# Constant products on TensorE at the head of each attention unit

## The chip, the cores and the metric

The kernel runs on one core of one Trainium2 chip. The metric is the time of one launch in microseconds of device time; lower is better. PE is TensorE, DVE is VectorE, ACT is ScalarE, POOL is GpSimd, SP is SyncE.

## What is computed

Three model blocks are applied one after the other to an activation of 1024 tokens by 1024 channels, in float32: an attention over chunks with a spatial gating unit, gates and a feed-forward; an mLSTM beside a windowed attention with a feed-forward; and a convolution beside a neighbourhood attention. The change touches the first and the third attention.

```python
# first block: 8 heads of 64, each chunk of 64 sees its own and 8 previous chunks
scores = jnp.einsum('bcqhd,bckhd->bhcqk', qc, kb).astype(jnp.float32) * (Dh ** -0.5)
scores = scores + bias[None, :, None, :, :]
scores = jnp.where(valid[None, None, :, None, :], scores, jnp.float32(-1e30))
probs = jax.nn.softmax(scores, axis=-1).astype(v.dtype)
out = jnp.einsum('bhcqk,bckhd->bcqhd', probs, vb)
...
# third block: 8 heads of 64, a grid of 16 rows by 64 columns, a window of 8 rows by 16 columns
s = jnp.einsum("bhwd,bhiwjd->bhwij", q_row, k_win).astype(jnp.float32) * scale
s = s + bias.transpose(0, 2, 1, 3).astype(jnp.float32)[None]
p = jax.nn.softmax(s.reshape(B, N_HEADS, GRID_W, kh * KW), axis=-1)
...
return jnp.einsum("bhwij,bhiwjd->bhwd", p, v_win)
```

## The kernel before

Activations are kept transposed, channels on partitions, as 8 tiles of 128 by 1024. A weight product is made of three products of rounded parts (w_hi with x_hi, w_hi with x_lo, w_lo with x_hi), so a *block* of 128 output features is 8 tiles by 3 parts by 2 halves of 512 tokens, 48 matmuls at line 389 (`feature_block`, `row_block`) or line 407 (`block_part`, a block cut in three). SP loads the weight blocks, POOL splits them into w_hi and w_lo, PE takes them in order.

PE writes into two accumulators, `acc[0]` and `acc[1]`, of 1024 columns each, in turn. `claim` waits until the accumulator of this turn has been taken, and `await_all_taken` until both have. The other half of PSUM holds `turned` (three banks for turned probabilities) and `att_out`.

Both attentions run over four *units* of two heads (a head pair). The names from here on:

- The **projections** of a unit are its weight blocks for v, q and k (and a gate in the third). ACT copies each from PSUM. In the third attention the units after the first also add eight row products of the unit before to `h` (`near_rows`, `add_rows`, line 897 on DVE).
- Then PE waits in `await_all_taken` until both accumulators are free: this is the **head pause**.
- `att_tensor` then runs over eight query tiles p = 0 to 7 of 128 queries. **S(p)** (line 709, `score`) is the scores of tile p for the two heads of the unit, one head per accumulator, on 64 rows of the array each. The number of keys is 128, 256, 384, 512 and then 640 in the first attention, and 512, 512, four times 576, and twice 512 in the third. **T(p)** (line 720, `turn_probs`) turns the probabilities, and **V(p)** (line 744, `weigh_values`) weighs the values with them. PE's order is S(0), S(1), T(0), S(2), T(1), V(0), S(3), T(2), V(1), and so on. At S(p+1) PE claims both accumulators, so it waits until DVE has taken both heads of S(p).
- DVE (`att_vector`) adds the bias and takes the row minimum (line 813, two of them per tile), ACT takes the exponential (line 854), DVE divides by the sum (lines 823 and 826), PE turns, ACT copies (line 864). DVE's own order is: scores of p, division of p, scores of p+1.
- After the last tiles a block of projections is cut into the pipeline to fill it (line 407).

DVE also works on the taps of the third block's convolution (line 1733), a fixed number of them between two units of the third attention.

TensorE's clock falls to half in stretches, which the profile lists. The kernel already has a function against that, `keep_clock`, that makes products of constants whose result nobody reads:

```python
def keep_clock(pe, n):
    for _ in range(n):
        pe.matmul(acc_all[:, 2 * TOK:2 * TOK + P], mean_w[:, :], ident[:, :], start=True, stop=True)
```

Both operands are 128 by 128 in float32, and the output is the first bank of `turned`. It is called at the norms, and at four other places between stages, and nowhere in the first or the third attention.

Of the kernel before, what the change touches and what calls it, by code (L numbers as in the profile page):

```python
# [155 lines left out]
def mixer_program(nc, x_t, blocks, n_blocks, params, consts, bias_1, bias_2, bias_3, sgu_rows, sgu_w, p_t,  # L156
                  out_t):

    with ExitStack() as ctx:
        def at(name, kib, shape, dtype=F32):  # L160
            return nc.alloc_sbuf_tensor_at(name, shape, dtype, offset=RESERVED + int(kib * 1024))
# [21 lines left out]
        def attention_buffers(base, kib, probs_kib, bias_kib, bias_width):  # L183
            return Buffers(
                q_t=at(base + "q_t", kib, [P, TOK]), k_t=at(base + "k_t", kib + 4, [P, TOK]),
                v_tok=at(base + "v_tok", kib + 8, [P, TT, P]), v_t=at(base + "v_t", kib + 12, [P, TOK]),
                scores=at(base + "scores", kib + 12, [P, 2, 640]),
                probs_t=at(base + "probs_t", kib + 17, [P, 2, 2, 5, P]),
                total=at(base + "att_sum", kib + 27, [P, TOK]), probs=at(base + "probs", probs_kib, [P, 2, 2, 640]),
                bias=at(base + "bias", bias_kib, [P, 2, bias_width]))  # L190

        band = attention_buffers("band_", 88, 152, 190, ATT_BIAS_1)
# [68 lines left out]
        near = Buffers(  # L261
            q_t=at("near_q_t", 140.625, [P, TOK]), k_t=at("near_k_t", 144.625, [P, TOK]),
            v_tok=at("near_v_tok", 148.625, [P, TT, P]), v_t=at("near_v_t", 156.625, [P, TOK]), scores=None,
            probs=at("near_probs", 152.625, [P, 2, 2, 640]), probs_t=at("near_probs_t", 162.625, [P, 2, 2, 5, P]),
            total=at("near_att_sum", 172.625, [P, TOK]), bias=None)
# [95 lines left out]
        def await_all_taken(e, t):  # L361

            for s in range(2):
                e.wait_ge(acc_free[s], t.count(f"acc{s}"))


        def take_block(pe, t):

            pe.wait_ge(w_split, t.next("block"))
            t.block += 1  # L370
            return (t.block - 1) % 2
# [25 lines left out]
        def feature_block(pe, t, parts_from=None):  # L397

            slot = take_block(pe, t)
            product(pe, t, [(slot, k, x_hi[:, k, :], x_lo[:, k, :]) for k in range(KT)], True, parts_from)  # L400
# [101 lines left out]
# [3 lines that stand above are left out]
# [175 lines left out]

        def att_tensor(pe, t, a, keys, next_block=True, joint=False):

            ahead = 1 if joint else 0

            def rows_of(side):
                return slice(64 * side, 64 * side + 64)

            def score(p):  # L690

                first, count, _ = keys(p)
                if joint:
                    s = claim(pe, t)
                    take_turn(pe, t)
                    for side in range(2):
                        ins = pe.matmul(acc[s][:, side * HALF:side * HALF + count],
                                        a.q_t[rows_of(side), p * P:(p + 1) * P],
                                        a.k_t[rows_of(side), first:first + count], start=True, stop=True)
                    ins.then_inc(acc_full[s], 1)  # L700
                    return
                slots = []
                for _ in range(2):
                    slots.append(claim(pe, t))
                    take_turn(pe, t)
                for c0 in range(0, count, 512):
                    c1 = min(count, c0 + 512)
                    for side in range(2):
                        ins = pe.matmul(acc[slots[side]][:, c0:c1], a.q_t[rows_of(side), p * P:(p + 1) * P],  # L709
                                        a.k_t[rows_of(side), first + c0:first + c1], start=True, stop=True)  # L710
                        if c1 == count:
                            ins.then_inc(acc_full[slots[side]], 1)

            def turn_probs(p):

                count = keys(p)[1]

                def turn(bank, side, c, at):
                    w = min(P, count - c * P)
                    return pe.transpose(turned[bank][0:w, at * P:(at + 1) * P],  # L720
                                        a.probs[:, p % 2, side, ahead + c * P:ahead + c * P + w], ident[:, :])

                for side in range(2):
                    pe.wait_ge(p_ready, t.next("p_ready"))
                    for _ in range(0 if p == 0 else 2 if side and keys(p - 1)[1] > HALF else 1):
                        pe.wait_ge(turned_copied, t.next("turned_copied"))
                    for c in range(min(4, -(-count // P))):
                        ins = turn(side, side, c, c)
                    ins.then_inc(turned_full, 1)
                if count > HALF:  # L730
                    for side in range(2):
                        ins = turn(2, side, 4, side)
                    ins.then_inc(turned_full, 1)

            def weigh_values(p):
                first, count, _ = keys(p)
                tiles = -(-count // P)
                if p == TT - 1:
                    for _ in range(3 if count > HALF else 2):
                        pe.wait_ge(turned_copied, t.next("turned_copied"))  # L740
                for c in range(tiles):
                    w = min(P, count - c * P)
                    for side in range(2):
                        ins = pe.matmul(att_out[rows_of(side), p % 4 * P:(p % 4 + 1) * P],  # L744
                                        a.v_tok[0:w, first // P + c, rows_of(side)],
                                        a.probs_t[0:w, p % 2, side, c, :], start=(c == 0), stop=(c == tiles - 1))
                if p % 4 == 3:
                    ins.then_inc(pv_done, 1)

            for n in range(ahead):  # L750
                score(n)
            for n in range(TT + 2):
                if n + ahead < TT:
                    score(n + ahead)
                if n == TT and next_block:
                    slot, s = take_block(pe, t), claim(pe, t)
                    take_turn(pe, t)
                    block_part(pe, t, slot, s, 0, 3)
                if 1 <= n <= TT:
                    turn_probs(n - 1)  # L760
                if n >= 2:
                    if n == TT + 1 and next_block:
                        block_part(pe, t, slot, s, 3, 4)
                    weigh_values(n - 2)
            if next_block:
                block_part(pe, t, slot, s, 4, KT)
# [137 lines left out]
        def projections_tensor(pe, t):  # L904

            turn_tiles(pe, t, band.v_t)
            feature_block(pe, t)
            await_all_taken(pe, t)

        def qkv_scalar(act, t, a):  # L910
# [6 lines left out]
        def att1_tensor(pe, t):  # L917
            feature_pair(pe, t, expect_parts(t, KT))
            with t.loop(2, acc0=20, acc1=20, block=6, p_ready=32, turned_copied=40, hi_ready=2, lo_ready=2):
                for _ in range(2):  # L920
                    projections_tensor(pe, t)
                    att_tensor(pe, t, band, keys_1)
                    feature_block(pe, t)
                    t.next("hi_ready")
                    t.next("lo_ready")
# [845 lines left out]
        def near_rows(pe, t):  # L1771
            await_parts(pe, t, 1)
            row_block(pe, t, [(near_hi[:, :], near_lo[:, :])])

        def near_tensor(pe, t):
            feature_block(pe, t)
            for n in range(HEAD_PAIRS):
                if n:
                    group_sums(pe, t, (n - 1, 0), n - 2 if n > 1 else None, near_square[:, :], t.next("squared"))
                feature_block(pe, t)  # L1780
                turn_tiles(pe, t, near.v_t)
                feature_block(pe, t)
                feature_block(pe, t)
                if n:
                    near_rows(pe, t)
                await_all_taken(pe, t)
                att_tensor(pe, t, near, keys_3)

        def conv_tensor(pe, t):
            last_near = t.next("squared")  # L1790
# [559 lines left out]
```

## Time and profile before

| | |
|---|---|
| median of 3 runs | 3624.6 us (3622.15 to 3625.77) |
| the profiled execution, its own time | 3623.64 us |
| its span | 3621.9 us |
| mean granted TensorE clock | 0.985 of full speed |
| PE busy | 3478.8 us (96%) |
| DVE busy | 1728.9 us (48%) |
| ACT busy | 797.4 us (22%) |
| POOL busy | 1201.0 us (33%) |

The span is the time from the first to the last instruction of one execution; the run's own time has 1.7 us more around it. Times in rows are us from the start of the span. The granted clock is 1.00 at 2.4 GHz and 0.50 at 1.2 GHz; there are no other levels in this trace. A row of the timeline merges instructions that follow each other, and its duration goes from the first one's start to the last one's modelled end.

### The profile page before, as it was taken

The numbers are of one execution on the slowest core, as the hardware profiler recorded it, in microseconds if no ns is written. First come the engines' busy times: TensorE is split into PE (matmuls) and PEld (weight loads), VectorE is DVE, ScalarE is ACT, GpSimd is POOL, SyncE is SP. The second block draws the span as 40 slices with busy tenths as digits, with TensorE's granted clock in tenths as the row PEclk, the third lists the DMA queues.
The fourth block names the chain that finished last, engine by engine and source line by source line (L and its number), as shares of the span: only waits on it lengthen the run. The fifth ranks groups of instructions, "written<-read, shape, count | busy, mean of one in ns | idle before, by whom it ended". The sixth has DMA issues, their size and how long they took to land.

```text
span 3621.9 us, 41941 instructions
## 1 busy us (share of the span) xinstructions
PE 3478.8 (96%) x16940; PEld 2772.5 (77%) x16940; DVE 1728.9 (48%) x2073; ACT 797.4 (22%) x1170; POOL 1201.0 (33%) x534
## 2 busy tenths in 40 slices
PE   7999999989999999989999999999999999999997
PEld 5767877778888888777876678888888868767675
DVE  4323433352323223588866642322322368888835
ACT  4433100020000000332234430000000141333452
POOL 2222344323433433333321134334333424222222
PEclk9999999999999999999999999999999999999998
DMA  2111211111111111122111011111111101111111
GB/s 95 39 36 38 93 47 46 47 35 47 46 52 46 46 52 46 35 66 81 59 34 33 23 41 47 52 46 46 52 46 58 47 18 60 59 60 58 44 35 64
DMA packets 52163, 178.96 MB, mean 49 GB/s; under 512 B 5728, under 2 KB 6368, under 8 KB 52064
## 3 DMA queue, kind: packets, MB, share of 16 engines
q1 hardware_dynamic: 38016, 138.43, 11.7%
q10 hardware_dynamic: 14048, 39.10, 3.2%
q8 instruction: 75, 1.23, 0.1%
q14 instruction: 24, 0.20, 0.0%
HBM read 172.79 MB, written 4.72 MB: 49 GB/s over the span
## 4 chain that ended last, share of the span: by engine, by line
PE 85%; DVE 8%; ACT 3%; issue 3%; POOL 1%; DMA 0%; ACTq 0%; DVEq 0%; POOLq 0%
PE acc L389 69%; PE acc L407 4%; PE acc L744 2%; PE acc L720 2%; PE acc L709 2%; PE acc L426 2%; DVE conv_slots L1733 1%; PE acc L473 1%; DVE rstd L618 1%; DVE normed L650 1%; DVE x_lo L488 0%; DVE h L897 0%; POOL w_lo L2060 0%; DVE window_scores L777 0%; PE acc L1355 0%
## 5 line engine op out<-in xcount | busy, mean ns | idle before, releaser
L2046 POOL TENSOR_TENSOR w_hi<-raw,zero 128x1024 fp32r<-128x1024 f32 x264 | 515.6, 1953 | 2365.2 <-PE acc L389 1663.1
L389 PE MATMUL acc<-x_hi,w_hi 128*128 128x512 f32 x2512 | 778.4, 391 | 5.7 <-POOL w_lo L2060 3.0
L389 PE MATMUL acc<-x_lo,w_hi 128*128 128x512 f32 x2512 | 774.2, 389 | 0.0
L389 PE MATMUL acc<-x_hi,w_lo 128*128 128x512 f32 x2512 | 774.0, 389 | 0.0
L2060 POOL TENSOR_TENSOR w_lo<-raw,w_hi 128x1024 fp32r<-128x1024 f32 x262 | 678.9, 2591 | 20.5
L897 DVE TENSOR_TENSOR h<-h,acc 128x1024 f32<-128x1024 f32 x312 | 380.7, 1221 | 554.9 <-PE acc L389 554.9
L389 PEld LDWEIGHTS acc<-x_hi,w_hi 128*128 128x128 f32 x2512 | 470.0, 188 | 106.7 <-POOL w_lo L2060 4.7
L389 PEld LDWEIGHTS acc<-x_lo,w_hi 128*128 128x128 f32 x2512 | 471.9, 188 | 98.7
L389 PEld LDWEIGHTS acc<-x_hi,w_lo 128*128 128x128 f32 x2512 | 471.8, 188 | 98.5
L1164 DVE TENSOR_TENSOR hid<-act_g,acc 128x1024 f32<-128x1024 f32 x44 | 53.7, 1221 | 570.7 <-PE acc L389 554.7
L483 ACT ACTIVATE hid_hi<-hid 128x1024 fp32r<-128x1024 f32 x44 | 46.7, 1061 | 909.2 <-DVE hid L1164 909.2
L1733 DVE SCALAR_TENSOR_TENSOR conv_slots<-conv_slots,par 128x1024 f32<-128x1024 f32 x120 | 227.8, 1898 | 4.1
L389 PE MATMUL acc<-hid_hi,w_hi 128*128 128x512 f32 x704 | 217.0, 389 | 0.7 <-DVE hid_lo L488 0.7
L389 PE MATMUL acc<-hid_lo,w_hi 128*128 128x512 f32 x704 | 216.7, 389 | 0.0
L389 PE MATMUL acc<-hid_hi,w_lo 128*128 128x512 f32 x704 | 216.7, 389 | 0.0
L488 DVE TENSOR_TENSOR hid_lo<-hid,hid_hi 128x1024 fp32r<-128x1024 f32 x44 | 138.2, 3140 | 49.9 <-ACT hid_hi L483 49.9
L389 PEld LDWEIGHTS acc<-hid_hi,w_hi 128*128 128x128 f32 x704 | 131.9, 188 | 28.5 <-DVE hid_lo L488 1.1
L389 PEld LDWEIGHTS acc<-hid_lo,w_hi 128*128 128x128 f32 x704 | 132.1, 188 | 27.5
L389 PEld LDWEIGHTS acc<-hid_hi,w_lo 128*128 128x128 f32 x704 | 132.1, 188 | 27.4
L1140 ACT ACTIVATE act_g<-acc 128x1024 f32<-128x1024 f32 x44 | 45.3, 1029 | 360.2 <-PE acc L389 360.1
L504 PEld LDWEIGHTS acc<-ident,mean_w 128*128 128x128 f32 x812 | 95.0, 194 | 21.0 <-issue 20.2
L504 PE MATMUL acc<-ident,mean_w 128*128 128x128 f32 x812 | 95.5, 278 | 16.2 <-DMA h<-x_t 16.2
(332 smaller groups left out, 4068.9 us busy)
## 6 DMA issues: line engine op xcount, KB each, us to landing
raw<-blocks SPq DMA_DIRECT2D x264, 512.0 KB, 3.4
near_bias<-bias ACTq DMA_DIRECT2D x16, 512.0 KB, 4.0
h<-x_t ACTq DMA_DIRECT2D x8, 512.0 KB, 8.2
h<-x_t ACTq DMA_DIRECT2D x1, 4096.0 KB, 15.5
q_past<-q_dram ACTq DMA_DIRECT2D x8, 512.0 KB, 5.6
w_own<-r_dram ACTq DMA_DIRECT2D x8, 512.0 KB, 6.5
out_t<-out_rows ACTq DMA_DIRECT2D x8, 512.0 KB, 3.0
band_bias<-bias ACTq DMA_DIRECT2D x4, 640.0 KB, 4.1
```

The costliest lines, as they stand in the source:

```text
L389: ins = pe.matmul(acc[s][:, c], w[:, slot, tile, :], part[:, c], start=(n == 0 and m == 0), stop=(n == last and m == 2))
L407: ins = pe.matmul(acc[s][:, c], w[:, slot, k, :], part[:, k, c], start=(k == 0 and m == 0), stop=(k == KT - 1 and m == 2))
L426: ins = pe.matmul(acc[accs[b]][:, c], w[:, slots[b], k, :], part[:, k, c], start=(k == 0 and m == 0), stop=(k == KT - 1 and m == 2))
L488: dve.tensor_tensor(lo, source, hi.bitcast(F32), ALU.subtract).then_inc(lo_ready, 1)
L504: pe.matmul(acc_all[:, 2 * TOK:2 * TOK + P], mean_w[:, :], ident[:, :], start=True, stop=True)
L709: ins = pe.matmul(acc[slots[side]][:, c0:c1], a.q_t[rows_of(side), p * P:(p + 1) * P], a.k_t[rows_of(side), first + c0:first + c1], start= ...
L720: return pe.transpose(turned[bank][0:w, at * P:(at + 1) * P], a.probs[:, p % 2, side, ahead + c * P:ahead + c * P + w], ident[:, :])
L744: ins = pe.matmul(att_out[rows_of(side), p % 4 * P:(p % 4 + 1) * P], a.v_tok[0:w, first // P + c, rows_of(side)], a.probs_t[0:w, p % 2, si ...
L897: dve.tensor_tensor(h[:, j, :], h[:, j, :], acc[s], ALU.add).then_inc(acc_free[s], 1)
L1733: ins = dve.scalar_tensor_tensor(out=out, in0=shifted, scalar=weight, in1=out, op0=ALU.mult, op1=ALU.add)
L2046: pool.tensor_tensor(hi, whole, nothing, ALU.add).then_inc(hi_split, 1)
L2060: pool.tensor_tensor(lo, whole, hi.bitcast(F32), ALU.subtract).then_inc(w_split, 1)
```

## The change

`att_tensor` takes a pair `idle`. After S(0) it makes `idle[0]` constant products and after S(1) `idle[1]`. Ahead of `await_all_taken`, in the head pause, come 12 products in the first attention and 10 in the third. The pairs are (9, 3) in the first and (18, 8) in the third. The second attention calls `att_tensor` with the pair (0, 0). No wait, semaphore, transfer or buffer changes. With four units in each attention this is 4 x (12 + 9 + 3) + 4 x (10 + 18 + 8) = 240 products more.

```diff
-        def att_tensor(pe, t, a, keys, next_block=True, joint=False):
+        def att_tensor(pe, t, a, keys, next_block=True, joint=False, idle=(0, 0)):
...
             for n in range(TT + 2):
                 if n + ahead < TT:
                     score(n + ahead)
+                if n < 2:
+                    keep_clock(pe, idle[n])
...
             turn_tiles(pe, t, band.v_t)
             feature_block(pe, t)
+            keep_clock(pe, 12)
             await_all_taken(pe, t)
...
                     projections_tensor(pe, t)
-                    att_tensor(pe, t, band, keys_1)
+                    att_tensor(pe, t, band, keys_1, idle=(9, 3))
...
                 if n:
                     near_rows(pe, t)
+                keep_clock(pe, 10)
                 await_all_taken(pe, t)
-                att_tensor(pe, t, near, keys_3)
+                att_tensor(pe, t, near, keys_3, idle=(18, 8))
```

## Rows read from the trace of the kernel before

**Rows 1.** The page: its first line, and the shares by engine of the chain that ended last.

```profile
span 3621.9 us, 41941 instructions
...
PE 85%; DVE 8%; ACT 3%; issue 3%; POOL 1%; DMA 0%; ACTq 0%; DVEq 0%; POOLq 0%
```

**Rows 2.** Windows: stretches of lowered clock in both attentions; stretch, busy us, granted clock.

```profile
74.09:80.92 6.83, 6.28 (x22) 2.41 (x20) 5.07 (x22) 3.58 (x14) 0.00 (x0) 0.50 0.01 2
...
207.21:210.62 3.41, 3.41 (x16) 1.51 (x12) 2.90 (x12) 2.27 (x10) 0.00 (x0) 0.50 0.00 0
...
3313.34:3320.17 6.83, 5.81 (x18) 3.00 (x20) 4.96 (x17) 4.00 (x10) 0.00 (x0) 0.50 0.39 99
...
sum 40.97, PE 36.73 PEld 17.75 DVE 31.17 ACT 21.73 POOL 0.00; mean PE 4.59 PEld 2.22 DVE 3.90 ACT 2.72 POOL 0.00
```

**Rows 3.** Groups by line, 740.7 to 745.5 us, where the kernel calls `keep_clock(pe, 20)`.

```profile
L504 PE MATMUL acc<-ident,mean_w 128*128 128x128 f32 x40 | 4.6, 275 | 0.0
```

**Rows 4.** Timeline of PE, third unit of the first attention: start, duration, [idle before].

```profile
200.95 0.61 PE L389 MATMUL acc<-x_lo,w_hi 128*128 128x512 f32 x2
201.40 0.61 PE L389 MATMUL acc<-x_hi,w_lo 128*128 128x512 f32 x2
203.22 0.49 PE L709 MATMUL acc<-band_k_t,band_q_t 64*128 64x128 f32 x4 [1.21 <-ACT band_k_t L914]
204.62 0.70 PE L709 MATMUL acc<-band_k_t,band_q_t 64*128 64x256 f32 x4 [0.91 <-DVE small L813]
...
206.75 1.24 PE L709 MATMUL acc<-band_k_t,band_q_t 64*128 64x384 f32 x4 [0.63 <-DVE small L813]
...
212.95 1.35 PE L709 MATMUL acc<-band_k_t,band_q_t 64*128 64x512 f32 x8 [0.34 <-DVE small L813]
...
216.30 1.35 PE L709 MATMUL acc<-band_k_t,band_q_t 64*128 64x512 f32 x8 [0.17 <-DVE small L813]
```

**Rows 5.** Timeline of DVE in the same unit.

```profile
203.94 0.35 DVE L813 CUSTOM_DVE_ANT_0 band_scores<-acc,band_bias,small 128x128 f32<-128x128 f32 x1
...
205.80 0.48 DVE L813 CUSTOM_DVE_ANT_0 band_scores<-acc,band_bias,small 128x256 f32<-128x256 f32 x1
```

**Rows 6.** Timeline of PE, first unit of the first attention: S(0) and S(4).

```profile
72.41 0.49 PE L709 MATMUL acc<-band_k_t,band_q_t 64*128 64x128 f32 x4 [1.21 <-ACT band_k_t L914]
...
82.93 1.35 PE L709 MATMUL acc<-band_k_t,band_q_t 64*128 64x512 f32 x8 [0.34 <-DVE small L813]
```

**Rows 7.** Timeline of PE, first unit of the third attention.

```profile
3120.97 0.61 PE L389 MATMUL acc<-x_hi,w_lo 128*128 128x512 f32 x2
3122.88 1.13 PE L709 MATMUL acc<-near_k_t,near_q_t 64*128 64x512 f32 x4 [1.30 <-ACT z_att L1831]
3125.85 2.08 PE L709 MATMUL acc<-near_k_t,near_q_t 64*128 64x512 f32 x4 [1.84 <-DVE small L813]
...
3129.78 1.30 PE L709 MATMUL acc<-near_k_t,near_q_t 64*128 64x512 f32 x8 [0.28 <-DVE small L813]
3131.14 1.11 PE L720 MATMUL acc<-ident,near_probs 128*128 128x128 f32 x8
...
3133.20 1.30 PE L709 MATMUL acc<-near_k_t,near_q_t 64*128 64x512 f32 x8
```

**Rows 8.** Timeline of DVE in the same unit: last division of tile 0, first scores of tile 1.

```profile
3126.82 0.49 DVE L826 TENSOR_SCALAR near_probs<-near_probs,small 128x512 f32<-128x512 f32 x1
...
3128.20 0.75 DVE L813 CUSTOM_DVE_ANT_0 near_probs<-acc,near_bias,small 128x512 f32<-128x512 f32 x1
```

**Rows 9.** Timeline of PE, third unit of the third attention: last row products, S(0) and S(3).

```profile
3309.35 0.63 PE L389 MATMUL acc<-near_hi,w_lo 128*128 128x512 f32 x2
3311.39 1.13 PE L709 MATMUL acc<-near_k_t,near_q_t 64*128 64x512 f32 x4 [1.40 <-DVE h L897]
...
3322.50 1.30 PE L709 MATMUL acc<-near_k_t,near_q_t 64*128 64x512 f32 x8
```

**Rows 10.** The chain that ended last, between two units of the third attention: start, us, what.

```profile
3182.77 1.87 DVE near_lo L488
3184.64 3.35 DVE conv_slots L1733
```

## The prediction, made before the change was run

> **What bounds the kernel now.** I read the page first. The chain that ended last is PE for 85% [rows 1], so PE time that is removed or added at a place where PE or its answer is waited for is removed from or added to the end. A change that adds work to PE alone and gives no shorter path of its own can only gain through the clock. So the second view is the granted clock. I cut the trace into its stretches of lowered clock: eight of them, one in each unit, lie in the two attentions, and together they last 40.97 us [rows 2]. In each unit the clock falls shortly after the head pause: PE has just waited for ACT or DVE, made the small S(0), and waited again for DVE, and then the clock is at 1.2 GHz for 3.41 or 6.83 us. The first attention has 6.83 twice and then 3.41 twice, the third 3.41 twice and then 6.83 twice. PE's work takes twice as long there, so no more than half of 40.97 us, 20.5 us, is to be had.
>
> The third view is the timeline of single heads, where one sees how long each pause is and who ends it. In the third unit PE's 512-column products come in pairs 0.45 us apart, so after the pair at 201.40 PE is free at 201.85, and S(0) starts at 203.22: a head pause of 1.37 us. S(0) holds PE for about 0.33 us (its four instructions last 0.49 to the modelled end), and S(1) starts 1.40 after S(0): a second pause of 1.07 us [rows 4]. The first unit of the third attention is free at 3121.42 and starts S(0) at 3122.88, a pause of 1.46 us. Its S(0) of 512 keys holds PE for about 0.97 us (1.13 to the end), and S(1) is 2.97 later: a second pause of 2.00 us [rows 7]. In the units after it PE is free at 3309.81 and starts at 3311.39, 1.58 us [rows 9].
>
> **What the change adds.** It removes and moves nothing. What counts is how long one constant product is. The kernel has the same call elsewhere: twenty products are 40 matmul instructions, since one float32 product of 128 columns is issued as two, and the 40 keep PE busy for 4.6 us with 0.275 for one [rows 3]. So they start (4.6 - 0.275) / 39 = 0.111 us apart, which with the rounding I take as 0.112, and one product is 0.224 us at full clock. At half clock it would be up to 0.448, but the clock is 1.00 when each head begins.
>
> The Trainium skill bears on this price. Its page TensorE: Matmul & The Clock Gate, section Back-to-back issue gap, gives 128 / 2.4 + 2.5 = 56 ns from one 128-column matmul to the next at 2.4 GHz, and by that all of these products would fit into their pauses. The row of this kernel has two instructions of 112 ns for each product, four times as much, and I go by the row.
>
> *Head pause.* 12 products are 2.69 us in a pause of 1.37: S(0) starts 1.32 us later. In the third attention 10 products are 2.24 us: 0.78 later in its first unit, 0.66 in each of the other three. ACT and DVE have long finished and wait, so nothing hides this. Sum: 4 x 1.32 + 0.78 + 3 x 0.66 = 8.0 us.
>
> *First attention from S(0) to S(4), at full clock throughout.* After S(0) come 9 products, 2.02 us, so S(1) starts at 0.33 + 2.02 = 2.35 instead of 1.40. S(1) lasts 0.70, and DVE starts on a result 0.23 us after it is there (203.94 against 203.71). So DVE takes the scores of tile 1 at 3.28, before at 2.58 [rows 4, 5], and S(2), which waits for both takings, moves by the same 0.70 from 3.53 to 4.23. The 3 products behind S(1) end at 2.35 + 0.53 + 0.67 = 3.55; T(0) fits in before S(2), so they are hidden. If DVE were faster they would cost up to 0.67. From S(2) on the pace is DVE's: S(1) to S(2) takes 2.13 for 128 columns divided and 256 scored, S(4) to S(5) takes 3.35 for 512 and 640. In between, by columns, S(2) to S(3) takes 2.54 and S(3) to S(4) 2.94 at full clock, an estimate from these two rows; with 3.41 us of half clock the two took 6.20 together. So S(4) is at 4.23 + 5.48 = 9.71. Before it was at 9.73 in the third unit [rows 4] and at 10.52 in the first [rows 6]; the second and the fourth are as their neighbours. Gain 0.8 twice and nothing twice: 1.6 us.
>
> *Third attention from S(0) to S(3).* 18 products are 4.03 us behind 0.97: S(1) at 5.00 instead of 2.97. S(1) holds PE until 5.97. 8 products, 1.79, end at 7.76, and T(0), eight turns at the 0.11 of [rows 7], at 8.64. Only then can S(2) start, before at 6.90. DVE is not the later one here: S(1) is there at 6.13, DVE starts at 6.36, and its two scorings with what lies around them took 1.58 (3128.20 to 3129.78), so the accumulators are free at 7.94 [rows 7, 8]. From S(2) PE makes S(2), T(1) and V(0) in a row, 3.42 us [rows 7], so S(3) is at 12.06. Before it was at 10.32 in the first two units and 11.11 in the third and fourth [rows 7, 9]. Loss 2 x 1.74 + 2 x 0.95 = 5.4 us.
>
> *Where it goes from there.* The first attention ends in PE's own blocks. Between units of the third the chain runs from PE's projections over ACT to the division and split on DVE and then over convolution taps [rows 10]; their number is fixed and they start when the attention has ended, so a late unit is late in full. Weights are no cover either: POOL and SP follow PE's use.
>
> **Sum.** 8.0 - 1.6 + 5.4 = 11.8 us. Against the profiled execution's own 3623.64 that is 3635.4; that execution lies 1.0 below the median of the runs, so by the median it is 3636.4. I predict 3636.4 us. "Same" means within 0.2%, 7.2 us, here and below, about what a measurement of this kernel can tell from no change.
>
> **Bounds of what the trace doesn't show.** How S(0) and the products follow each other (64 rows, then 128) is in no row; at each of the 16 places it can cost nothing or, an estimate, one more start of an instruction, 0.11 us: 0 to 1.8 us. I take nothing. The clock's return is worth between nothing (the DVE pace of 6.20 stays: 3 us more in the first attention) and what DVE's pace allows. Where the lowered stretches fall differs by execution; each unit has 3.41 or 6.83. If all eight had 6.83, before would be about 3 us longer and so the loss smaller. My own range for the forecast is 3631 to 3641.
>
> **Rivals.**
>
> *The products fit, and the clock's gain is what remains (faster).* For this a product must cost what one instruction does, 0.112 us: 12 of them are 1.34 in 1.37, 9 are 1.01 in 1.07, 10 are 1.12 in 1.46, and 18 are 2.02 in 2.00. Then S(4) in the first attention is at 3.53 + 5.48 = 9.01, a gain of 1.5 twice and 0.7 twice, 4.4 us. In the third DVE is free at 3126.82 + 0.49, 4.43 after S(0) [rows 8], takes tile 1 about then, S(2) follows 1.58 later at 6.05 and S(3) at 9.47: a gain of 0.85 twice and 1.64 twice, 5.0. Together 9.4 us: 3615.2. It turns at about 0.17 us for a product. For it speaks that 12, 9 and 18 at 0.112 fill the pauses to within 0.07 us; against it [rows 3]. By the 56 ns of the Trainium skill's page TensorE: Matmul & The Clock Gate the time would be this one too. Chance 0.10.
>
> *The loss is partly absorbed (same).* The clock falls less elsewhere, or DVE catches up in the 576-key tiles of the third attention, where PE and DVE end almost together. If half of the 5.4 us there and 3 of the first attention come back, 3630. Chance 0.17.
>
> *The clock falls all the same, only later in the unit (slower still).* PE still has pauses around S(2) and S(3) of the first attention, of 0.63 before S(2) [rows 4]. Then the change pays for the products and gives back none of the 9.4 us: about 3645. Against it: in all eight units the fall comes right behind the pauses that are now filled. Chance 0.10.
>
> That leaves 0.63 for the forecast. Faster by over 0.2% is the first rival, 0.10. Same gets the second rival and a little of the low end of the forecast, 0.19; slower the rest, 0.71. The range reaches down to the absorbed loss and up towards the third rival: 3626 to 3643.
>
> **What the profile after would show.** Groups of line 504 with 24, 18 and 6 instructions in the first attention and 20, 36 and 16 in the third, 480 more in all, 0.112 apart. S(0) directly behind them, without idle time. S(1) 2.35 after S(0) in the first attention and 5.0 in the third. No stretch of lowered clock between S(0) and S(4). S(4) at 9.7 and S(3) at 12.1. A T(0) in the third attention that starts at 7.8 and an S(2) that waits for nothing. The prediction is wrong if a product takes one instruction, if the clock still falls, or if S(3) of the third attention isn't later than 11.

## The result, and the profile after

| | median | range | ratio to the kernel before, 95% interval |
|---|---|---|---|
| before | 3622.73 us | 3619.8 to 3625.77, 6 runs | |
| changed | 3636.23 us | 3634.75 to 3637.99, 6 runs | 1.0037 (1.0024 to 1.005) |

The change makes the kernel slower by 13.5 us, 0.37%, clear of 0.2%; the prediction was 3636.4 us. The profiled execution took 3634.75 us, 11.1 more than that of before. One execution of the kernel third_no_s1 below took 10783 us where the six others took 3631 to 3636; it is left out, and every other execution counts. The page after, its first lines and the chain that ended last [rows 1]:

```profile
span 3633.0 us, 42901 instructions
...
PE 3510.3 (97%) x17420; PEld 2815.3 (77%) x17420; DVE 1727.1 (48%) x2073; ACT 797.5 (22%) x1170; POOL 1201.4 (33%) x534
...
PE 86%; DVE 7%; issue 3%; ACT 3%; POOL 1%; DMA 0%; ACTq 0%; DVEq 0%; POOLq 0%
```

PE has 17420 matmul instructions, before 16940: the 240 products are 480 instructions, and as many weight loads. The chain is a little more PE.

The windows of the eight units from S(0) on (stretch, us, PE busy, granted clock), where there were eight lowered stretches [rows 2]:

```profile
74.00:84.50 10.50, 9.71 (x67) 1.00 0.01 3
140.40:150.90 10.50, 9.71 (x67) 1.00 0.00 0
206.90:217.40 10.50, 9.70 (x67) 1.00 0.01 2
273.30:283.80 10.50, 9.70 (x67) 1.00 0.00 0
3127.00:3140.00 13.00, 13.00 (x103) 1.00 0.31 87
3223.40:3236.40 13.00, 13.00 (x104) 1.00 0.29 86
3319.70:3332.70 13.00, 13.00 (x104) 1.00 0.30 87
3417.90:3430.90 13.00, 13.00 (x104) 1.00 0.29 88
```

The clock is at 2.4 GHz in all eight. The change does what it says, and in the windows of the third attention PE has no idle time left at all. What fills it is the products. The timeline of PE in the first unit of the first attention [rows 6]:

```profile
74.02 0.49 PE L709 MATMUL acc<-band_k_t,band_q_t 64*128 64x128 f32 x4
74.44 2.27 PE L504 MATMUL acc<-ident,mean_w 128*128 128x128 f32 x18
76.64 0.70 PE L709 MATMUL acc<-band_k_t,band_q_t 64*128 64x256 f32 x4
77.28 0.94 PE L504 MATMUL acc<-ident,mean_w 128*128 128x128 f32 x6
78.05 0.38 PE L720 MATMUL acc<-ident,band_probs 128*128 128x128 f32 x2
78.54 0.92 PE L709 MATMUL acc<-band_k_t,band_q_t 64*128 64x384 f32 x4
...
81.07 1.13 PE L709 MATMUL acc<-band_k_t,band_q_t 64*128 64x512 f32 x4 [0.34 <-DVE small L815]
```

S(1) now comes 2.62 us after S(0) and waits for nothing but the 18 instructions in front of it. And in the first unit of the third attention [rows 7]:

```profile
3127.03 1.13 PE L709 MATMUL acc<-near_k_t,near_q_t 64*128 64x512 f32 x4
3128.08 4.29 PE L504 MATMUL acc<-ident,mean_w 128*128 128x128 f32 x36
3132.30 1.13 PE L709 MATMUL acc<-near_k_t,near_q_t 64*128 64x512 f32 x4
3133.36 2.05 PE L504 MATMUL acc<-ident,mean_w 128*128 128x128 f32 x16
3135.25 1.04 PE L720 MATMUL acc<-ident,near_probs 128*128 128x128 f32 x8
3136.21 1.30 PE L709 MATMUL acc<-near_k_t,near_q_t 64*128 64x512 f32 x8
...
3139.52 1.30 PE L709 MATMUL acc<-near_k_t,near_q_t 64*128 64x512 f32 x8
```

S(1) is 5.27 after S(0), before 2.97. S(2) is at 9.18, before at 6.90, right behind T(0) and without any wait.

### The profile page after: what moved, and what is told of

Same layout as the page of the kernel before. It is cut to its first block, busy times and chain, and to the rows that moved or that the text cites. A ratio compares the mean times of both kernels' runs of the same rounds, so it can differ in the third digit from the quotient of the medians.

```text
span 3633.0 us, 42901 instructions
## 1 busy us (share of the span) xinstructions
PE 3510.3 (97%) x17420; PEld 2815.3 (77%) x17420; DVE 1727.1 (48%) x2073; ACT 797.5 (22%) x1170; POOL 1201.4 (33%) x534
## 4 chain that ended last, share of the span: by engine, by line
PE 86%; DVE 7%; issue 3%; ACT 3%; POOL 1%; DMA 0%; ACTq 0%; DVEq 0%; POOLq 0%
PE acc L389 70%; PE acc L407 4%; PE acc L744 2%; PE acc L720 2%; PE acc L504 2%; PE acc L426 1%; PE acc L473 1%; PE acc L709 1%; DVE rstd L618 1%; DVE normed L650 1%; DVE conv_slots L1736 1%; DVE x_lo L488 0%; POOL w_lo L2064 0%; DVE window_scores L779 0%; PE acc L1358 0%
## 5 line engine op out<-in xcount | busy, mean ns | idle before, releaser
L504 PEld LDWEIGHTS acc<-ident,mean_w 128*128 128x128 f32 x1292 | 150.9, 193 | 29.9 <-issue 27.9
L504 PE MATMUL acc<-ident,mean_w 128*128 128x128 f32 x1292 | 154.5, 278 | 16.6 <-DMA h<-x_t 16.6
```

## The experiments

Ten kernels. Each differs from the changed kernel only in the counts, or in what a product is, and each was run beside the kernel before on the same chip. The counts are written as head pause, (behind S(0), behind S(1)), for the first and for the third attention. In the changed kernel they are 12, (9, 3) and 10, (18, 8).

| kernel | first | third | median us | its kernel before | ratio, 95% interval |
|---|---|---|---|---|---|
| fit | 5, (3, 1) | 6, (8, 4) | 3612.4 | 3622.49 | 0.9971 (0.9962 to 0.9981) |
| turns | 12, (9, 3), half price | 10, (18, 8), half price | 3612.79 | 3622.49 | 0.9974 (0.9965 to 0.9984) |
| head_only | 12, (0, 0) | 10, (0, 0) | 3622.9 | 3622.49 | 1.0003 (0.9993 to 1.0012) |
| scores_only | 0, (9, 3) | 0, (18, 8) | 3627.04 | 3622.49 | 1.0013 (1.0003 to 1.0022) |
| third_no_s1 | 12, (9, 3) | 10, (18, 0) | 3632.51 | 3621.79 | 1.0031 (1.0019 to 1.0043) |
| first_only | 12, (9, 3) | none | 3626.47 | 3621.79 | 1.0011 (1.0002 to 1.002) |
| fit_no_s1 | 5, (3, 0) | 6, (8, 0) | 3610.95 | 3621.79 | 0.997 (0.9959 to 0.9981) |
| fit_first | 5, (3, 1) | none | 3617.04 | 3621.79 | 0.9985 (0.9976 to 0.9994) |
| fit_head | 5, (0, 0) | 6, (0, 0) | 3615.36 | 3622.44 | 0.9982 (0.9973 to 0.9991) |
| fit_s0 | 0, (3, 0) | 0, (8, 0) | 3609.08 | 3622.44 | 0.9964 (0.995 to 0.9977) |

**fit: as many products as the pauses hold.**

```diff
-            keep_clock(pe, 12)
+            keep_clock(pe, 5)
...
-                    att_tensor(pe, t, band, keys_1, idle=(9, 3))
+                    att_tensor(pe, t, band, keys_1, idle=(3, 1))
...
-                keep_clock(pe, 10)
+                keep_clock(pe, 6)
...
-                att_tensor(pe, t, near, keys_3, idle=(18, 8))
+                att_tensor(pe, t, near, keys_3, idle=(8, 4))
```

> The change with fewer products, so many as go into each pause at 0.224 us each and 0.1 us at each turn between 64 and 128 rows: 5, (3, 1) in the first attention and 6, (8, 4) in the third. My theory (the loss is the products' overrun, and the clock's return is worth 9.4 us): no stretch of lowered clock in the eight units, S(0) and S(1) where they were before (S(1) 1.40 and 2.97 after S(0)), S(4) of the first attention at 9.0 and S(3) of the third at 9.5, and 9.4 us less than the kernel before, about 3613. Rival (the clock's return is worth next to nothing, since DVE sets the pace): within 2 us of the kernel before. Rival (fewer products don't hold the clock): stretches of lowered clock stay, 3618 to 3623.

Measured 3612.4, 10.1 less than before. In the first unit of the third attention:

```profile
3119.21 1.13 PE L709 MATMUL acc<-near_k_t,near_q_t 64*128 64x512 f32 x4
3120.27 2.05 PE L504 MATMUL acc<-ident,mean_w 128*128 128x128 f32 x16
3122.25 1.13 PE L709 MATMUL acc<-near_k_t,near_q_t 64*128 64x512 f32 x4
...
3125.28 1.30 PE L709 MATMUL acc<-near_k_t,near_q_t 64*128 64x512 f32 x8
...
3128.70 1.30 PE L709 MATMUL acc<-near_k_t,near_q_t 64*128 64x512 f32 x8
```

S(1) is at 3.04 and S(3) at 9.49; in the first attention S(4) is at 9.0 in all four units. The granted clock is 1.00 from S(0) on in the windows of all units. By its trace S(4) and S(3) of the eight units are 8.8 us earlier together than before, 4.2 in the first attention and 4.6 in the third. So the clock's return is real and worth about what the estimate of 9.4 said, and the rival by which DVE's pace hides it falls.

**turns: the same counts at half the price.** The constant product becomes a transposition of the same constant, which is one instruction. `keep_clock` elsewhere stays as it is.

```diff
+        def turn_clock(pe, n):
+            for _ in range(n):
+                pe.transpose(acc_all[:, 2 * TOK:2 * TOK + P], mean_w[:, :], ident[:, :])
...
-                    keep_clock(pe, idle[n])
+                    turn_clock(pe, idle[n])
...
-            keep_clock(pe, 12)
+            turn_clock(pe, 12)
...
-                keep_clock(pe, 10)
+                turn_clock(pe, 10)
```

> The change with the same counts, but each product of the heads is a transposition of the same constant by the identity, one matmul instruction instead of two. So the price of a product is halved and nothing else. My theory: 0.11 us each, the pauses are filled but not overrun by more than 0.2 us, and if transpositions hold the clock the time is 9 us below the kernel before, about 3614. If they don't hold it, the clock falls as in the kernel before and the time is that of the kernel before, 3623. The Trainium skill, TensorE: Matmul & The Clock Gate, part 4, says that the clock doesn't rise for transpositions; by that the second. Rival (the loss isn't the products' length but the interruption of the scores by other weights): 3630 or more.

Measured 3612.79, 9.7 less than before. Same places, same counts and same order, and the loss is gone. PE in the first unit of the third attention, and the windows of that unit and of the first unit of the first attention:

```profile
3118.58 1.25 PE L508 MATMUL acc<-ident,mean_w 128*128 128x128 f32 x10
3120.04 1.13 PE L713 MATMUL acc<-near_k_t,near_q_t 64*128 64x512 f32 x4 [0.21 <-ACT z_att L1839]
3121.10 2.18 PE L508 MATMUL acc<-ident,mean_w 128*128 128x128 f32 x18
3123.21 1.13 PE L713 MATMUL acc<-near_k_t,near_q_t 64*128 64x512 f32 x4
```

```profile
73.00:83.00 10.00, 8.70 (x57) 1.00 0.01 2
...
3120.00:3130.00 10.00, 9.89 (x76) 1.00 0.40 113
```

Eighteen products are 2.18 us here and 4.29 in the changed kernel. This is the prediction's first rival made true: at one instruction each the counts fit, and the time is 9.7 us below its kernel before, where that rival had 9.4. The clock holds. This kernel changes the kind of instruction together with its price. That the kind isn't what matters is seen in fit, where the products are those of the changed kernel, only fewer, and the gain is about the same, 10.1.

**head_only and scores_only: the two parts of the change.** In the first the pairs are (0, 0), in the second the two calls in the head pause are left out.

> Only the products of the head pause (12 and 10), the pairs are (0, 0). My theory: S(0) is late by what it is late in the changed kernel, 1.42 us in the first attention and 0.88 and 0.76 in the third, 8.8 us together. If the clock then holds, its 9.4 us come back and the time is about that of the kernel before (3622). If the clock still falls behind S(0), 3631. Rival (the products behind S(0) and S(1) cost nothing since DVE is waited for there): the whole loss is here, about 3636.

> Only the products behind S(0) and S(1), (9, 3) and (18, 8), none in the head pause. My theory: S(0) not late; S(4) of the first attention at 10.0, S(3) of the third at 12.5, as in the changed kernel, if the clock holds: 7.2 us more than before, about 3630. If the clock still falls in some units, 2 us more for each pair of them. Rival (the loss is all in the head pause): at or below the kernel before.

head_only measured 3622.9: the overrun of the head pause and the clock's return cancel, as the theory says. In its trace the clock still fell in two of the eight units, for 3.4 us each:

```profile
209.80:213.20 3.40, 3.40 (x14) 1.51 (x12) 2.72 (x12) 2.08 (x9) 0.00 (x0) 0.50 0.00 0
3220.30:3223.70 3.40, 3.33 (x14) 2.45 (x14) 3.05 (x10) 2.17 (x6) 0.00 (x0) 0.50 0.63 178
```

scores_only measured 3627.04, 4.6 more than before (an interval of about 1 to 8 us) where 7.2 was expected. Its S(0) isn't late and S(4) and S(3) are at the 10.0 and 12.5 of the changed kernel, so the 7.2 are there in its heads, and they lie inside the interval. The two results, 0.4 and 4.6, don't add up to 13.5, because each part alone already brings the clock back and so has the gain of about 9.4 us in it; the whole change has it once. Their sum with 9.4 added is 14.4, near the 13.5. Both parts thus cost time. Neither rival, which put all of it into one of them, holds, but that of scores_only is excluded by the lower end of the interval alone, 1 us.

**first_only: the change in the first attention alone.**

```diff
-                keep_clock(pe, 10)
...
-                att_tensor(pe, t, near, keys_3, idle=(18, 8))
+                att_tensor(pe, t, near, keys_3)
```

> The change in the first attention alone: 12 and (9, 3). My theory: S(0) 1.42 late in each of four units, S(7) 0.26 us early in all of them together against the kernel before: 5.4 us more, about 3628. The rest of the change, 8 us, is the third attention's. Rival (most of the loss is in the first attention's head pause, the most overrun one): 3633 or more.

Measured 3626.47, 4.7 more than before (expected 5.4). By the medians the larger part of the loss, 8.8 us, is the third attention's.

**third_no_s1: without the 8 products behind S(1) of the third attention.**

```diff
-                att_tensor(pe, t, near, keys_3, idle=(18, 8))
+                att_tensor(pe, t, near, keys_3, idle=(18, 0))
```

> The changed kernel without the 8 products behind S(1) in the third attention: the pair (18, 0). My theory: those 8 products and T(0) stand in front of S(2) and set it at 9.19 after S(0). Without them DVE sets it: S(1) at 5.27 is there at 6.40, DVE starts at 6.69, S(2) at 8.27. So 0.9 us less in each unit, 3.7 us in all, about 3632.5. Rival (the products behind S(1) are hidden behind DVE, and the third attention's loss is the 18 alone): 3636, as the changed kernel.

Measured 3632.51, which is 10.7 above its kernel before, against 13.5 for the changed kernel: 2.8 less, where 3.7 was expected. The two intervals overlap, so the times alone don't show this difference; the trace does:

```profile
3131.51 1.13 PE L709 MATMUL acc<-near_k_t,near_q_t 64*128 64x512 f32 x4
3132.57 1.09 PE L720 MATMUL acc<-ident,near_probs 128*128 128x128 f32 x8
3134.51 1.30 PE L709 MATMUL acc<-near_k_t,near_q_t 64*128 64x512 f32 x8 [0.85 <-DVE small L815]
```

S(2) waits for DVE again, at 8.27 after S(0) (3126.24 here), as expected, and S(3) is at 11.70 instead of 12.50, in all four units, 3.2 us together. The products behind S(1) were not hidden.

**fit_first: the fitted counts in the first attention alone.**

> The fitted counts in the first attention alone: 5, (3, 1). My theory: S(4) at 9.0 in all four units, the first attention's share of the clock's return, 4.4 us of 9.4: about 3618. Rival (the first attention gives back nothing since DVE sets its pace): 3622.5, and all of the fitted kernel's 10 us are the third's.

Measured 3617.04, 4.75 less than before. That leaves 5.3 of fit's 10.1 for the third attention; the estimate had 4.4 and 5.0. The rival, which had nothing for the first attention, is outside the interval of about 2 to 9 us. How large the shares are isn't shown any closer by the times; S(4) is at 9.0 in all four units, as in fit.

**fit_no_s1, fit_head, fit_s0: which pause has to be filled.**

> The fitted counts without the products behind S(1): 5, (3, 0) and 6, (8, 0). Theory A (the head pause and the pause behind S(0) are what brings the clock down): it holds as in the fitted kernel, 3612. Theory B (the products behind S(1) are needed too): the clock falls in some units behind S(1), 3.4 us at a time with some 0.7 us of loss each, 3613 to 3618.

> The fitted counts of the head pause alone: 5 and 6, pairs (0, 0). Theory A (either pause left open brings the clock down in a part of the units, by where it falls in time): lowered stretches in two to four of the eight units, each worth 0.7 to 1.6 us, about 3613 to 3617. Theory B (the pause behind S(0) alone decides): the clock falls in all eight and the time is that of the kernel before. Theory C (the head pause alone decides): 3611.

> The fitted counts behind S(0) alone: (3, 0) and (8, 0), nothing in the head pause. Theory A: lowered stretches in some of the units, 3612 to 3616. Theory B (the pause behind S(0) alone decides): none, 3611. Theory C (the head pause alone decides): as the kernel before.

fit_no_s1 measured 3610.95 and has no lowered stretch in the units: theory A of its expectation holds, and the products behind S(1) are for nothing. fit_head measured 3615.36, and in its trace the clock still falls in three of the eight units:

```profile
76.80:83.60 6.80, 6.18 (x22) 0.50 0.00 1
206.50:213.30 6.80, 6.31 (x21) 0.50 0.00 0
3404.80:3408.20 3.40, 3.40 (x12) 0.50 0.59 172
```

fit_s0 measured 3609.08, 13.4 less than before, with the fewest products of all: 3 behind S(0) in the first attention and 8 in the third, 44 in all. From S(0) on its clock stays up:

```profile
73.50:83.50 10.00, 8.46 (x50) 1.00 0.01 2
201.50:211.50 10.00, 8.51 (x52) 1.00 0.00 0
3118.00:3128.00 10.00, 9.04 (x66) 1.00 0.40 111
3399.20:3409.20 10.00, 9.06 (x66) 1.00 0.37 112
```

So in these traces filling the pause behind S(0) is enough, and filling the head pause is neither needed nor enough. With that pause filled none of the eight units fell, in scores_only neither; with the head pause alone filled three of eight fell in one trace, two of eight in another. For fit_s0 theory B holds, for fit_head theory A, so neither theory is right as it stood: filling the head pause helps in most units, filling the pause behind S(0) in all. There is one trace of each. That fit_s0 is faster than fit_no_s1 or fit by more than noise isn't shown: their intervals overlap, that of fit_s0 goes from 8 to 18 us below its kernel before, and in its trace S(4) and S(3) stand where they stand in fit.

## Why the prediction was right

**The price of a product.** Taken as two instructions 0.112 us apart. The 36 instructions of the third attention last 4.29 us, where 35 starts and one duration of 0.275 make 4.20. Right, and with the turns kernel it decides the sign: halving it turns +13.5 into -9.7.

**The head pause.** Predicted S(0) later by 1.32 us in the first attention and by 0.78 and 0.66 in the third, 8.0 in all; measured 1.42, 0.88 and 0.76, 8.8 in all. The missing 0.1 at each place lies where scores on 64 rows follow weights on 128.

**The first attention from S(0) to S(4).** S(1) was predicted at 2.35 and came at 2.62; S(2) 4.23 and 4.52; S(4) 9.71 and 10.00. From S(2) to S(4) the estimate by columns gave 5.48, the trace has 5.48. So the only error after the change is the 0.28 around the group behind S(0), for which the prediction had named the place and had taken nothing. The trace has it as longer starts: 0.21 from the first product behind S(0) to the next instruction, and 0.21 from the last one to S(1), in place of 0.11. With the 0.1 of the head pause it is 0.38 in a unit, 3.0 us in all, beyond the bound of 0 to 1.8 that was put on it. A smaller error was in the state before: the second unit was taken to be like the first, and its S(4) was at 10.29, not 10.52. So S(0) to S(4) gained 0.25 us in all, not 1.6.

**The third attention from S(0) to S(3).** S(1) 5.00 and 5.27, S(2) 8.64 and 9.18, S(3) 12.06 and 12.49. That S(2) would wait for T(0) and not for DVE was right: it has no idle time in front of it, and third_no_s1 gives it the wait for DVE back. The size is off by 0.43 in a unit; 0.27 of it is there at S(1) already, around the group behind S(0).

**The clock's return.** Put at 9.4 us; fit, which has little but this, measured 10.1 and turns 9.7.

**The sum.** With what the trace of after has, the terms are 8.84 - 0.25 + 7.42 = 16.0 us for the two attentions; predicted were 11.8. The two spans differ by only 11.1. The rest, -4.9, is outside the heads. One part is the clock there: where the stage times lie after the change, the clock falls at other moments. Windows of four stretches of work with such falls, before and then after:

```profile
770.00:800.00 30.00, 24.22 (x118) 0.89 0.06 18
...
2085.00:2105.00 20.00, 14.23 (x53) 0.91 0.08 26
2975.00:3000.00 25.00, 19.65 (x99) 0.86 0.06 22
3525.00:3560.00 35.00, 25.95 (x82) 0.80 0.05 15
```

```profile
780.00:810.00 30.00, 24.05 (x98) 0.94 0.05 18
...
2089.00:2109.00 20.00, 14.45 (x53) 0.83 0.10 26
2979.00:3004.00 25.00, 18.93 (x108) 1.00 0.07 22
3536.00:3571.00 35.00, 25.26 (x86) 0.90 0.04 15
```

Three of the four have a higher clock after and one a lower; at 2979 to 3004 the fall is gone. In two more such stretches it was 0.83 and 0.89 before and is 0.89 and 0.91 after. By the places of the heads in both traces 2.3 us of the rest lie between the two attentions and 1.0 behind the last unit, where these stretches are; that the clock makes up all of these 3.3 us isn't shown. The other part, 1.7, is between the first two units of the third attention: DVE's busy time on the convolution's taps there is 42.83 us for 22 of them before and 41.10 for 22 after:

```profile
3149.00:3216.50 67.50, 42.83 (x22) 1.00 0.17 55
```

```profile
3155.30:3221.10 65.80, 41.10 (x22) 1.00 0.19 56
```

Why the taps were slower before isn't shown. The prediction named where lowered stretches fall as a thing that differs by execution and put a price on it for the heads alone; a clock that falls less elsewhere it had only in its second rival.

That it met the median within 0.2 us is therefore luck in good part, and three errors make it up. The terms were 4.2 us too small: 16.0 in the trace against 11.8. If the heads' 16.0 hold in each execution, the medians, 13.5 apart, say that what lies outside them gave 2.5 back; how much of the 4.9 lasts from one execution to the next wasn't measured apart. The profiled execution was the fastest of its six and had the highest mean granted clock, 0.994 where the others had 0.991 and 0.992. And the base was 1.9 too high: the forecast stood on 3624.6, the median of three executions, and the six of the result have 3622.73. As a loss, 11.8 was predicted and 13.5 measured.

**The rivals.** That products fit is false for this kernel and true for turns. That the loss is partly absorbed didn't occur in the heads, where DVE caught up nothing in the 576-key tiles: S(7) of the third attention is as late as S(3). Outside the heads it did in this pair of traces, by the part of the 4.9 us that the clock gave, though not so far that the time stayed the same. That the clock falls all the same didn't occur in any of eight units. What the prediction held against this, that every fall comes right behind the pauses now filled, was read too closely: in the third unit of the first attention the fall begins at 207.21, after S(2) at 206.75 [rows 2, 4]. That filling an earlier pause is enough there too is what fit_s0 showed.

## What to carry to other kernels

Before filling an engine's pause, read in the trace what one filler costs in instructions, for this data type, and how long the pause is from the end of the last work to the release, with the changes between fillers and work in it; a filler that overruns a pause on the critical chain is paid in full, and 24 products in a unit were 5.4 us of PE for pauses of 2.4. A held clock is worth only what PE sets: here 41 us of half clock were worth about 10, since DVE set much of the pace. Try the smallest fill first, at one pause at a time: 44 products held the clock in all eight units, and by the medians gave no less than the 108 of fit.

## What the runs showed of the hardware

- A group of products on all 128 rows between scores on 64 rows costs more than its own starts: S(1) comes 0.28 us later than 18 starts of 0.112 say in the first attention and 0.27 in the third.
- Transpositions kept the clock up as well as products did: in the turns kernel the granted clock is 1.00 in the windows from S(0) on of all eight units. The Trainium skill, TensorE: Matmul & The Clock Gate, Part 4, says that the full clock doesn't engage for transpositions; by that this kernel should have been as slow as before, and the measurement goes the other way. They stood among other matmuls here; a stretch of transpositions alone wasn't tried.
- In the fit_head trace the clock fell in the third unit of the first attention and not in the second, although the instructions and the pauses of both are the same. Whether it falls thus depends on more than the instructions around it, and with the pause behind S(0) left open some units fall and others don't.
